# Old cache rows copied partly beside the mixer, samples' first loads and the first transposed m issued earlier, in a gated hybrid decoder step

## The reference

```
xn = _rmsnorm(x, g_pre);  u = xn @ w_in
o_a, s_new = _gla(q, k, v, log_a, gla_s0)
y_a = (rmsnorm(o_a) * silu(gg)) @ w_gla_branch
...                                  # for each window g = 128, 512, 2048 rows:
    kk = concatenate([buf[:, :, 0], k]);  vv = concatenate([buf[:, :, 1], v])
    o, lse = softmax attention of the 8 new tokens over strided rows of kk, vv
    new_buf = stack([kk, vv])[:, Lb + T - keep:]      # the old cache, shifted by 8 rows
y_b = (combination of the groups' o by softmax(lse) * silu(dg)) @ w_dil_branch
merged = sigmoid(ga) * y_a + sigmoid(gb) * y_b
h = x + _rmsnorm(merged @ w_out, g_post)
h = h + (pe @ w_ple_proj) * sigmoid(h @ w_ple_gate)
```

## Time and profile before

| | |
|---|---|
| median of 3 runs | 2817.8 us |
| the profiled execution's own time | 2818.61 us |
| its span | 2816.8 us |
| PE busy | 2778.1 us (99% of the span) |
| PEld, DVE, ACT, POOL busy | 52%, 38%, 31%, 14% |
| queue q1 (issued by SP) | 296.86 MB, 35.1% of 16 engines' span |
| queue q0 (issued by POOL) | 258.89 MB, 27.5% |
| mean DMA rate | 198 GB/s |

### The profile page before, as it was taken

How to read it: one execution, slowest core, us unless ns; L and a number is a source line. 1 busy time by engine, 2 the same in 40 slices (tenths; PEclk the granted TensorE clock), 3 DMA queues, 4 the chain that set the end, 5 groups by cost and what they waited for, 6 DMA issues and landing times.

```text
span 2816.8 us, 40869 instructions
## 1 busy us (share of the span) xinstructions
PE 2778.1 (99%) x16168; PEld 1458.2 (52%) x16168; DVE 1080.3 (38%) x2401; ACT 871.9 (31%) x1788; POOL 386.1 (14%) x633
## 2 busy tenths in 40 slices
PE   8999999999999999999999989999999899999998
PEld 4444456555545665666555545555544344444444
DVE  6311134444333443344223323333323455555452
ACT  5211034444312222333123321111113444444341
POOL 2000010111311002120011113232200000000000
PEclk9999999999999999999999999999999999999999
DMA  9543454655677566584576759787736966556642
GB/s 282 132 169 130 149 202 151 215 189 202 202 250 275 178 193 205 188 276 157 179 266 219 242 174 326 238 261 244 235 136 199 308 170 174 142 159 178 163 113 57
DMA packets 320399, 558.36 MB, mean 198 GB/s; under 512 B 179114, under 2 KB 184305, under 8 KB 316242
## 3 DMA queue, kind: packets, MB, share of 16 engines
q1 hardware_dynamic: 269154, 296.86, 35.1%
q0 software_dynamic: 51056, 258.89, 27.5%
HBM read 378.96 MB, written 236.79 MB: 219 GB/s over the span
## 4 chain that ended last, share of the span: by engine, by line
PE 95%; DMA 2%; SPq 2%; DVE 1%; issue 0%; POOL 0%; ACT 0%; POOLq 0%; DVEq 0%
PE out L2614 42%; PE out L2183 22%; PE out L2611 15%; PE out L1120 2%; PE out L1105 2%; PE out L2617 2%; PE out L1111 1%; PE out L614 1%; PE out L625 1%; PE out L624 1%; PE out L1403 1%; PE out L1096 1%; PE out L1363 1%; DMA U<-stage 1%; SPq L355 1%; DMA sw_kc<-in_cache_kv_w 0%
## 5 line engine op out<-in xcount | busy, mean ns | idle before, releaser
L2614 PE MATMUL out<-w_hi,xn_hi 128*128 128x512 f16 x1920 | 729.0, 380 | 1.3 <-DVE w_lo L2483 0.7
L2614 PE MATMUL out<-w_lo,xn_hi 128*128 128x512 f16 x1920 | 728.3, 379 | 0.0
L2614 PE MATMUL out<-w_hi,xn_lo 128*128 128x512 f16 x1920 | 728.2, 379 | 0.0
L2514 ACT ACTIVATE stage<-out 128x512 f32<-128x512 f32 (+1 forms) x170 | 99.3, 584 | 900.0 <-PE out L2614 605.4
L2552 DVE TENSOR_SCALAR stage<-out 128x512 f32<-128x512 f32 (+1 forms) x170 | 114.8, 676 | 646.9 <-PE out L2614 424.1
L2614 PEld LDWEIGHTS out<-w_hi,xn_lo 128*128 128x128 f16 x1920 | 188.0, 98 | 227.0 <-issue 0.8
L2614 PEld LDWEIGHTS out<-w_hi,xn_hi 128*128 128x128 f16 x1920 | 188.4, 98 | 207.7 <-issue 6.5
L2614 PEld LDWEIGHTS out<-w_lo,xn_hi 128*128 128x128 f16 x1920 | 188.1, 98 | 200.8 <-issue 0.5
L2611 PE MATMUL out<-xn_hi,w_hi 128*128 128x512 f16 x640 | 242.8, 379 | 0.0
L2611 PE MATMUL out<-xn_hi,w_lo 128*128 128x512 f16 x640 | 242.6, 379 | 0.0
L2611 PE MATMUL out<-xn_lo,w_hi 128*128 128x512 f16 x640 | 242.6, 379 | 0.0
(11 more groups left out here) (318 smaller groups left out, 4007.5 us busy)
## 6 DMA issues: line engine op xcount, KB each, us to landing
out<-in_cache_kv_w POOLq DMA_DIRECT2D x64, 1020.0 KB, 9.6
U<-stage SPq DMA_DIRECT2D x240, 256.0 KB, 4.7
raw<-in_w_in SPq DMA_DIRECT2D x78, 512.0 KB, 5.0
sw_kc<-in_cache_kv_w POOLq DMA_DIRECT2D x24, 1024.0 KB, 12.0
sw_vc<-in_cache_kv_w POOLq DMA_DIRECT2D x24, 1024.0 KB, 9.9
UT<-stage SPq DMA_DIRECT2D x80, 256.0 KB, 3.7
sw_rows<-U POOLq DMA_DIRECT2D x32, 512.0 KB, 7.2
out<-in_cache_kv_w POOLq DMA_DIRECT2D x16, 1008.0 KB, 7.6
```

The costliest lines, as they stand in the source:

```text
L2514: move_out(act, m, lambda o, x: act.activation(o, x, ACT.Copy, scale=1.0 / W_SCALE))
L2614: last = pe.matmul(out[m % 3][:, :], x[:, k, at:at + P], y[:, k, :], start=first, stop=final)
```

## The change

Five edits. (1) `shift` is issued once instead of twice or once in every eighth slot, until 45 pieces are left; three of these go out in each of the mixer's turns 1 to 15, behind POOL's small work of the turn. (2) The first loads of `Samples` are issued from slot 515 instead of 522, behind `head_done` of the last head but one (its results stored) instead of both; the mask's load, and the wait for the last head, move to slot 527. The buffers are allocated in another order, so that what is loaded at 515 lies in the first set's memory and the rest (`sw_vc`) in the second's. (3) DVE waits by `read` until the last head's results are in `result`, not until they are stored. (4) SP turns the first m right behind the second z, ahead of pe and of tile 2's loads. (5) `queue_weights` goes from SP's queue to ACT's, in the same slot and with the same wait.

```
-        self.qT = [sb(f"qT{s}", [P, SEQ]) for s in range(2)]
+        self.result, self.qT, self.k, self.v = zip(*[(... one set's four tiles ...) for s in range(2)])
...
+    def head_done(self, eng, g, h):
+        eng.wait_ge(self.summed, (g * HEADS + h + 1) * BLOCKS)
+        eng.wait_ge(self.stored[h % 2], self.moved(g, h))
+    def read(self, eng):
+        eng.wait_ge(self.summed, GROUPS * self.STEPS)
+        eng.wait_ge(self.result_kept, GROUPS * self.STEPS)
...                                                       # Samples: sw_kc, sw_new_k, sw_new_v, sw_q, sw_rows, then sw_vc
-        if r == -5:
+        if r == -12:
             self.load_q(q, 0)
             for p in range(last + 1):
                 self.load_k(q, 0, p)
...
+        if r == 0:
             q.dma_start(self.mask[:, :], self.mask_in).then_inc(self.mask_loaded, 16)
...
         if slot == self.MERGE_SLOT + 1:
             self.turn_z(sp, 1)
+            self.turn_m(sp, 0)
             self.turn_pe(sp, 1)
             self.load_early(sp, 2)
...
         if slot == self.MERGE_SLOT + 2:
-            self.turn_m(sp, 0)
...
-            if slot == SAMPLE_SLOT - 5:
+            if slot == SAMPLE_SLOT - 12:
+                windows.head_done(q, GROUPS - 1, HEADS - 2)
+                cutter.done(q)
+            if slot == SAMPLE_SLOT:
                 windows.done(q)
-                cutter.done(q)
...                                                       # sync
-                if m == COLUMN_TILES * TOKEN_TILES - 1 and half == 1:
-                    for i in range(2):
-                        sp.wait_ge(out_ready[i], COLUMN_TILES * TOKEN_TILES // 2)
-                    mix.queue_weights(sp)
...                                                       # scalar
+                    if half == 1 and m == COLUMN_TILES * TOKEN_TILES - 1:
+                        for i in range(2):
+                            act.wait_ge(out_ready[i], COLUMN_TILES * TOKEN_TILES // 2)
+                        mix.queue_weights(act)
...                                                       # gpsimd, MIX_PIECES = 3
-                if n >= 1 and at % 8 == 6 and pieces:
+                if n >= 1 and at % 8 == 6 and len(pieces) > MIX_PIECES * (mix.TURNS - 4):
                     pool.wait_ge(lo_ready, min((n + 1) * PIECES + at // 8 + 1, COLUMN_TILES * PIECES))
-                    count = 2 if at < TOKEN_TILES - 1 else 1
-                    for piece in pieces[:count]:
-                        shift(*piece)
-                    pieces = pieces[count:]
+                    shift(*pieces.pop(0))
...
             for t in range(1, mix.TURNS):
                 mix.pool(pool, t)
+                for piece in pieces[:MIX_PIECES]:
+                    shift(*piece)
+                pieces = pieces[MIX_PIECES:]
...                                                       # vector, slot 525
-                    windows.done(dve)
+                    windows.read(dve)
```

More of the change, by code:

```diff
@@ L186 @@
 SHIFT_PIECES = ((128, 1), (512, 2), (2048, 8))
+MIX_PIECES = 3
 SHIFTS = DEC_BATCH * sum(n for _, n in SHIFT_PIECES) * 16
@@ L982, in __init__ @@
         self.U, self.UT, self.mask_in, self.identity, self.OG = U, UT, mask_in, identity, OG
-        self.qT = [sb(f"qT{s}", [P, SEQ]) for s in range(2)]
+        self.result, self.qT, self.k, self.v = zip(*[(sb(f"result{s}", [P, BLOCKS, HD + 2]), sb(f"qT{s}", [P, SEQ]), sb(f"k{s}", [P, BLOCKS, HD]),
+                                                      sb(f"v{s}", [P, BLOCKS, HD])) for s in range(2)])
         self.query = [sb(f"query{s}", [P, SPAN]) for s in range(2)]
-        self.k = [sb(f"k{s}", [P, BLOCKS, HD]) for s in range(2)]
-        self.v = [sb(f"v{s}", [P, BLOCKS, HD]) for s in range(2)]
         self.kT = sb("kT", [P, BLOCKS, P])
-        self.result = [sb(f"result{s}", [P, BLOCKS, HD + 2]) for s in range(2)]
         self.mask = sb("mask", [P, 2, P])
@@ L1077, in left @@
                                            self.prob_turned, self.prob_kept, self.summed, self.result_kept)]
+    def head_done(self, eng, g, h):
[4 more added lines that the diff above has]
+        eng.wait_ge(self.result_kept, GROUPS * self.STEPS)
     def done(self, eng):
-        wait(eng, self.summed, GROUPS * self.STEPS)
-        for h in range(HEADS - 2, HEADS):
-            wait(eng, self.stored[h % 2], self.moved(GROUPS - 1, h))
+        self.head_done(eng, GROUPS - 1, HEADS - 2)
+        self.head_done(eng, GROUPS - 1, HEADS - 1)
     def at(self, g, i):
@@ L1187, in __init__ @@
         self.kc = sb("sw_kc", [P, N_CACHE, WIDTH])
-        self.vc = sb("sw_vc", [P, N_CACHE, WIDTH])
         self.new_k = sb("sw_new_k", [P, WIDTH])
@@ L1192, in __init__ @@
         self.q_places = [(tile, QUAD) for tile in (self.new_k, self.new_v, sb("sw_q", [P, WIDTH]))]
+        self.rows = [sb(f"sw_rows{s}", [P, self.PAIR, WIDTH]) for s in range(self.RING)]
+        self.vc = sb("sw_vc", [P, N_CACHE, WIDTH])
         self.qT = sb("sw_qT", [P, GROUPS * HEADS, QUAD])
         self.kT = [sb(f"sw_kT{s}", [P, HEADS, P]) for s in range(2)]
-        self.rows = [sb(f"sw_rows{s}", [P, self.PAIR, WIDTH]) for s in range(self.RING)]
         self.sT = [sb(f"sw_sT{i}", [P, P]) for i in range(len(ROWED))]
@@ L1294, in queue @@
                 if p == 0:
-                    for x in range(self.RING):
+                    for x in range(3):
                         self.load_rows(q, x)
+        if r == 0:
             q.dma_start(self.mask[:, :], self.mask_in).then_inc(self.mask_loaded, 16)
@@ L2464, in _ @@
                     mix.norm_a(pool, 2)
-            assert not pieces
             for t in range(1, mix.TURNS):
                 mix.pool(pool, t)
+                for piece in pieces[:MIX_PIECES]:
+                    shift(*piece)
+                pieces = pieces[MIX_PIECES:]
+            assert not pieces
             pool.wait_ge(copied, SHIFTS + 4 * GROUPS * 16)
```

## The result

The changed kernel takes 2861.7 us in the median of 12 runs, from 2819.3 to 2914.7; the kernel before took 2818.1 (2816.0 to 2823.2). The comparison uses only the executions near each kernel's fastest, so its ratio of 1.0068, 95% interval [1.0041, 1.0095], is the loss at its mildest; the medians are 43.6 us apart. The spread is part of the finding: the kernel before has a spread of 7 us, this one of 95.

The account below looks back on a forecast made before the run. PE bounds the kernel, busy 2778.1 of 2816.8 us, so only 38.7 us idle and some half clock can be won. 2818.61 - 10.1 - 4.4, copies 0, less 0.8 for the median: 2803 us, range 2796 to 2810.

Parts of the forecast that it names:

- The samples' first loads: Start of the samples: loads go out some 49 us sooner, PE's 8.1 us wait and 2.0 of half clock go, 10.1 us.
- The change of stages: Around `out(0)` and the third z: weights 4.9 us sooner, net 2.5, plus z's 1.9 us wait gone, 4.4 us.
- rival A: Change of stages: weights in by about 2188, before the clock falls, or PE never stops; 2795.3 to 2797 us, chance 0.19.
- the first term: Samples' old-key loads issued sooner: 8.1 us of PE wait plus 2.0 us of half clock won, 10.1 us.
- rival B: Change of stages: weights' larger rows win the engines, tile 2's loads and z come late; 2808 us, chance 0.18.
- if both queues progress alike: Change of stages: SP's 4.47 MB and ACT's 4.19 MB share 419 GB/s, all in 20.7 us later, at 2189.1.
- Two terms of the sum: Third z: rows ready at 2189.7; SP's stores through by 2189.8, so z turned by 2198 and the 1.92 us wait goes.
- The copies in steady turns: Mixer turns: three copies add 8.7 us to 23.3 us of DMA time in 38.8 us, so they fit; cost 0.
- Even pushed back by all 8.7 us they hold: Steady mixer turns: h's transposes are issued 25.6 us before `gate` needs them, so 8.7 us of copies cause no stop.
- the small packets are not held behind 65 KB ones: Queues sharing an engine: read from 494 GB/s at 160 to 162 us, a copy beside stores and loads.
- Rival C: Mixer turns: copies stretch transposes by over 25.6 us, h late every turn, 2 us stop each; 2833 us, chance 0.06.

Follow-up runs that it names:

- e8: Changed kernel without copies beside the mixer, tile 2's inputs loaded ahead of m's transposes, gate's weights issued by ACT only after the third z: 2806.7 us, ratio 0.9957.

## Why the prediction was wrong, step by step

**The samples' first loads: right, to the tenth.** No wait for `sw_kc`, granted clock 1.00 in both stretches, and PE begins the mixer at 2160.01 where the kernel before began it at 2170.12: 10.1 us, as forecast. That it fits to the tenth is luck: in the other kernels with these loads the mixer begins 8.0 to 10.4 us sooner.

**The change of stages: 4.4 us forecast, 1.4 measured.** The weights were not 3.3 us late but in time, which was the condition of rival A (its "490 GB/s" counts from 2170.3; from 2168.4, where the forecast's own sum starts, it is 442). It was z that was late. Its products begin 13.4 us sooner (2195.35 for the earlier trace rows's 2208.74), but run at half clock until about 2199, a loss of 1.9; less the first term's 10.1, 1.4 is left. Without the copies nothing is left of it: the mixer begins 9.6 us sooner there, and the span is 9.2 us shorter in all. This is rival B's mechanism, and its 2808 is near the 2809.3 of that kernel. ACT's and DVE's rows:

```profile
2160.18 0.34 ACTq L1802 DMA_DIRECT2D mix_w_hi<-CUT_HI  x1
2160.55 0.51 ACTq L1802 DMA_DIRECT2D mix_w_lo<-CUT_LO  x1
```

```profile
2178.11 0.17 DVE L2053 TENSOR_TENSOR mix_least<-mix_og 128x4 f32<-128x4 f32 x1 [17.56 <-DMA mix_pe_in<-in_p_prompt]
```

The step that failed is "if both queues progress alike". They progress alike in packets: from 2166 to 2168 the records have 48 packets of SP's ring (88 KB) and 45 of ACT's (737 KB), and from 2164 to 2178, seven such stretches, 355 and 357. It is so from the start: in each half microsecond from 2161.5 to 2163.5 SP's ring has 44 to 50 packets of 4 KB, in the two from 2164 to 2165 it has 7 and 7, beside 9 and 12 of ACT's 16 KB. I had put this rival at 0.18 on the strength of a stretch that showed no such pair. Two terms of the sum fell with it, both given here in the changed kernel's time, 10.1 us sooner than the prediction's: z's rows were to be ready at 2179.6 and were at 2189.3; the last stores to U were to let SP go at 2179.7 and did at 2187.33. The second would have held z without the first: with the rows ready at 2173.7, z still waited 9.1 us (e8). Rival B named only the first.

The Trainium skill (DMA: Bandwidth & Descriptors, "Queues, rings and completion order") says that an engine goes round its queues and takes a whole packet, typically of 9 to 17 descriptors, from one before it turns to the next. The 355 to 357 agree with the round; but the counts come near each other within half a microsecond, so here the change comes after each packet of the records, which is one row of 1 to 16 KB. (The records do not name the engine; the alternation is read from these counts.) I gave the rule less weight than a row that did not bear on it.

**The copies in steady turns: 0 forecast, and this is what decided.** The failed sentence is "Even pushed back by all 8.7 us they hold". It adds the copies' own engine time to the turn's; but beside transposes their time isn't additive. m's lo transpose took up to 37.6 us to issue, over the 25.6 I had named as cover for h. The support, "the small packets are not held behind 65 KB ones", came from 160 to 162 us, with loads and stores of kilobytes beside a copy. It could show nothing on transposes: in the whole trace of before, no 256-byte packet starts while a copy's packet is open. I also followed the wrong victim: POOL issues the copies behind `norm_m`, and SP has m's lo transpose in hand at that moment, 0.9 us after them:

```profile
2396.61 1.61 POOL L2438 DMA_DIRECT2D out<-in_cache_kv_w  x3 [0.21 <-issue]
```

```profile
2397.51 22.14 SPq L1791 DMA_TRANSPOSE mix_mTl<-mix_m_rowl  x1
```

**Rival C had the mechanism, and not the size or place.** It asked for h late in every turn and gave 2833; m was late, in six of the tiles by 8.2 to 23.8 us. Between them are turns in which nothing is lost (no stop from 2224.84 to 2421). That such turns are more or fewer from one execution to the next would explain why one kernel takes 2819 or 2915; it is not shown, since one execution was profiled. At 0.06 it had far too little: its own evidence, 6.50 us of issue for 1.92, was with the earlier trace rows all there was about transposes beside other traffic, and I set it aside because a steady turn's mean share was 0.60.

## What to carry to other kernels

A transfer "beside" others isn't priced by its share of engine time: ask which packets of which ring it meets. Keep large-row copies off a second ring while another ring issues transposes that something waits for; on the transposes' ring, behind h's, the same bytes were free, and in small rows they cost 8.8 us. And when a load's wait is moved by reordering, follow the issuing engine's own waits down to the next one: here the weights' wait became z's, and when z's rows came sooner, z's wait was SP standing for a store.

## What the runs showed of the hardware

- SP's and ACT's rings pass packets in like numbers: 355 to 357 in 14 us, rows of 1 to 4 KB against 16 KB, so the bytes go by the size of the rows.
- A share of 1.01 can mean 82 GB/s. The share of a DMA engine counts the time that a packet is open, not bytes moved.
- Beside 65280-byte packets of another ring, a transposing packet of 256 bytes took 97 to 1379 ns in the mean of a stretch, for 22 alone: most took 18 ns, and one in six (163 of 975) over 1 us. In 4096-byte packets the same copies cost 8.8 us in a whole kernel.
- On one ring large packets and transposing ones pass in order: transposes issued at 2511.60 started at 2520.4, behind three copies, and PE had no wait for them.
